# Moving one ScalarE instruction within the delta stage: a head's high half before the next head's squares, weight split and tanh

## What is computed

```
qkv = silu(causal_depthwise_conv(proj[..., :3 * DN_WIDTH], conv_w))      # 4 taps
q, k = l2_normalize(q), l2_normalize(k)                                  # 8 heads of 128
# per head, in chunks of 64 tokens in the reference:
lower = where(strict, (k * beta) @ k.T * decay, 0)
u, w  = triangular_solve(lower + I, [v * beta, k * beta * exp(gc)])
v_new = u - w @ state
o     = (q * exp(gc)) @ state + attn @ v_new
state = state * exp(gc_last) + k_dec.T @ v_new
o     = o * rsqrt(mean(o * o) + eps) * norm_w * silu(z)
y     = o @ w_out
```

## Time and profile before

| | us |
|---|---|
| median of 3 runs | 1089.87 (1088.97 to 1091.43) |
| the profiled execution | 1092.04 |
| its span, first to last instruction | 1090.2 |
| TensorE busy with matmuls | 1064.6 |
| DVE, ACT, POOL busy | 611.7, 473.7, 483.9 |

### The profile page before, as it was taken

One profiled execution on the slowest core, in us unless ns is written; L12 is line 12 of the kernel. 1 busy time (PEld: TensorE's weight loads), 2 busy tenths in 40 slices (PEclk: granted clock), 3 DMA queues, 4 the chain that ended last, 5 costly groups with the idle time before them and its releaser, 6 DMA issues. The chain is left out here.

```text
span 1090.2 us, 16275 instructions
## 1 busy us (share of the span) xinstructions
PE 1064.6 (98%) x5659; PEld 878.4 (81%) x5659; DVE 611.7 (56%) x1365; ACT 473.7 (43%) x1057; POOL 483.9 (44%) x276
## 2 busy tenths in 40 slices
PE   7999999999999999999999999999999999999997
PEld 6888888888878888888888888877788887766775
DVE  6777747767646646512122126436956767644677
ACT  6654346566543431531331333343334444454544
POOL 5786413332436775774574575346222122113230
PEclk9999999999999999999999999999999999999999
DMA  6554431221106154354343543514112011000011
GB/s 214 145 136 130 109 97 49 78 58 50 56 25 209 49 174 156 96 174 135 116 154 102 149 154 97 150 27 110 40 39 68 21 39 49 20 20 11 20 69 78
DMA packets 167157, 100.08 MB, mean 92 GB/s; under 512 B 30424, under 2 KB 160812, under 8 KB 166060
## 3 DMA queue, kind: packets, MB, share of 16 engines
q1 hardware_dynamic: 166924, 99.06, 31.3%
q10 hardware_dynamic: 160, 0.07, 0.0%
HBM read 95.69 MB, written 3.16 MB: 91 GB/s over the span
## 5 line engine op out<-in xcount | busy, mean ns | idle before, releaser
L1260 POOL TENSOR_TENSOR wlo<-stage,whi 128x1024 fp32r<-128x1024 f32 (+1 forms) x105 | 274.5, 2618 | 215.8 <-ACT whi L763 215.4
L2272 PE MATMUL ps<-hhi,whi 128*128 128x512 f32 (+1 forms) x728 | 306.9, 422 | 1.9 <-DVE gated L2033 0.9
L2272 PE MATMUL ps<-hhi,wlo 128*128 128x512 f32 (+1 forms) x728 | 296.7, 408 | 0.0
L2272 PE MATMUL ps<-hlo,whi 128*128 128x512 f32 (+1 forms) x728 | 288.5, 400 | 0.0
L2272 PEld LDWEIGHTS ps<-hhi,whi 128*128 128x128 f32 (+1 forms) x728 | 137.0, 188 | 36.1 <-issue 5.4
L1358 POOL TENSOR_TENSOR wlo<-stage,whi 128x1024 fp32r<-128x1024 f32 (+3 forms) x40 | 73.3, 1835 | 205.5 <-ACT whi L1050 205.5
L763 ACT ACTIVATE whi<-stage 128x1024 fp32r<-128x1024 f32 x104 | 109.7, 1056 | 120.7 <-PE ps L2272 88.8
L2272 PEld LDWEIGHTS ps<-hhi,wlo 128*128 128x128 f32 (+1 forms) x728 | 137.2, 188 | 30.1 <-issue 6.6
L2272 PEld LDWEIGHTS ps<-hlo,whi 128*128 128x128 f32 (+1 forms) x728 | 137.1, 188 | 26.2 <-issue 1.9
L2272 PE MATMUL ps<-ahi,whi 128*128 128x512 f32 x312 | 124.1, 398 | 3.4 <-POOL alo L1310 3.4
L1138 ACT ACTIVATE prob<-ps,aneg 128x128 f32<-128x128 f32 (+1 forms) x96 | 50.7, 528 | 168.8 <-DVE aneg L2064 122.9
(11 more groups left out here) (399 smaller groups left out, 1765.2 us busy)
## 6 DMA issues: line engine op xcount, KB each, us to landing
stage<-dn_w_in SPq DMA_DIRECT2D x32, 512.0 KB, 4.2
stage<-mlp_w_up SPq DMA_DIRECT2D x32, 512.0 KB, 4.6
stage<-mlp_w_down SPq DMA_DIRECT2D x32, 512.0 KB, 4.6
mod_w<-ada_w SPq DMA_DIRECT2D x8, 1536.0 KB, 6.6
stage<-w_in SPq DMA_DIRECT2D x17, 512.0 KB, 3.6
gcrow<-gc_rows SPq DMA_DIRECT2D x16, 256.0 KB, 3.7
stage<-dn_w_out SPq DMA_DIRECT2D x8, 512.0 KB, 3.4
stage<-w_in SPq DMA_DIRECT2D x9, 256.0 KB, 3.0
```

Of the source, the lines that this page charges most:

```text
L1260: pool.tensor_tensor(wlo[:, slot, 0:ks, 0:cols], stage[:, slot, 0:ks, 0:cols], whi[:, slot, 0:ks, 0:cols], ALU.subtract).then_inc(s["w_lo" ...
L2272: mm = pe.matmul(bank, w[:, slot, k - ks[0], 0:width], x[:, k], start=(i == 0), stop=(i == len(todo) - 1))
```

## The change

In ScalarE's order of a head, `out_hi(h - 1)` is moved in front of `q_squares(g)`, `next_split(f"v{g}")` and `conv_tanh(f"v{g}")`. It acts in heads 1 to 6: head 0 has no head before it, and head 7 has its own place for it. No instruction is added or removed, and the programs of the other engines are unchanged.

```diff
@@ -977,11 +977,11 @@
                 v_new(h, 3)
                 o_first(h, 3)
                 if ahead:
+                    if h:
+                        out_hi(h - 1)
                     q_squares(g)
                     next_split(f"v{g}")
                     conv_tanh(f"v{g}")
-                    if h:
-                        out_hi(h - 1)
                 o_squares(h, 2)
                 o_squares(h, 3)
                 if g + 1 < H:
```

## The result

The changed kernel takes 1104.86 us, median of five runs (1103.83 to 1106.38), against 1091.3 us for the kernel before (five runs, 1088.97 to 1091.56). The ratio is 1.0127, 95% interval 1.0115 to 1.0138: 1.3% slower, 13.9 us at the median of before. The profiled execution has a span of 1103.1 us, 12.9 more than before. The five runs of before have a median 1.4 us above that of the three from which the forecast was made.

A forecast was written before the change was run, and what follows sets the result against it. TensorE, its matmul row busy 1064.6 of 1090.2 us, was taken as the bound. Heads 1 to 5 (11.35 us) and head 6 (0.4) gave 11.7; 1089.87 + 11.7 = 1101.6 us, 1.1% slower, range 1096.5 to 1105.

The forecast's parts named there:

- ScalarE's order, +0.52 us: In heads 1 to 6 the moved out_hi makes squares, weight's high half and tanh each start 0.52 us later, uncovered before vT.
- The hold of vT: On DVE, vT waits for POOL's subtraction wlo, started 0.48 us earlier, taking 2.44 us instead of 0.69; 1.75 us a head.
- Heads 1 to 5, 5 x 2.27: Delta stage, heads 1 to 5: each period longer by 1.75 + 0.52 = 2.27 us, 11.35 us in all.
- Head 6, +0.4 us: In head 6 TensorE's 1.6 us loss on alo goes, but late vT opens a somewhat larger hole: +0.4 us.
- (a): Rival: vT is not held and the tanh's 0.52 us finds cover; only head 6's hole goes, 1088.3 us; chance 0.05.
- (b): Rival: no hold of vT, only the longer chain, 5 x 0.52 and head 6's -1.6 + 0.5: +1.5, 1091.4 us; chance 0.07.
- (c): Rival: vT held in every head, but the next head wins back the tanh's shift: +8.7, 1098.6 us; chance 0.08.
- (d): Rival: the edit does not act, as ScalarE waits for gf in the new place; chance below 0.01.
- the cost of the clock: Over head 0's TensorE hole the granted clock was read as staying 1.00, 2.4 GHz; the sum had no clock term.
- the upper bound of 1105: Whole kernel: at most 13.6 us lost, 6 heads at 2.27 without the 1.6 us recovered, plus the spread of before.
- The starting point, 1089.87 us: Median of three runs of the kernel before, to which the forecast added its 11.7 us.

The follow-up runs named there:

- the run with two halves: The changed kernel, but POOL makes the low half of the weight of v in two instructions of 128x512 in heads 1 to 6: 1098.92 us, ratio 1.0072.

## Why the prediction was right, and where it fell short

**ScalarE's order, +0.52 us.** Right. Alone it costs 0.54 us a head, by the run with POOL's start put late.

**The hold of vT, 1.75 us a head, out of head 0's row.** Right, by three runs: without the hold 1.73 come back, with the hold alone 1.78 are lost, and with one operand in PSUM it does not happen. vT was forecast to end 0.56 us behind wlo, and does; had all of its 0.69 us followed the release, heads would be 23.67 us long and not 23.54. That is how the prediction read the Trainium skill (SBUF — State Buffer, section SBUF: two separate sides); the measurement decides for 0.56.

**Heads 1 to 5, 5 x 2.27.** The first four are 2.24 to 2.28 us longer; the fifth is 3.13 longer, 0.85 of it the clock.

**Head 6, +0.4 us.** The stretch from 302.46 to 315.17 is 12.71 us against 12.34: +0.37. The wait on alo is gone, the one on vT stands in its place. The prediction counted only the wait on alo for TensorE in 165 to 300 us; the same view has 1.1 us on vT too, head 0's, which it had put into that head's period, so the sum is not touched.

**The rivals.** (a) gave 1088.3 us and (b) 1091.4; the run that removes the hold has (b)'s form, +1.5 us forecast and +1.5 measured by the medians (1.9 by the ratio, 0.5 to 3.2), and shows that the order without its hold would have cost about what (b) said. (c), 1098.6 us, fails by the periods, since nothing wins back the 0.52. The edit did act, so (d) fails.

**The step that failed is the cost of the clock.** I read from head 0 that the granted clock stays 1.00 over a hole of 1.2 us and put its cost at nothing; the sum had no term for it, and neither had the upper bound of 1105, made from holes and the spread of before. One head's clean row was taken for a rule, and it was one draw: behind the same hole the clock did fall in the run with POOL put late, and that head took 0.96 us more. In the two profiles the stretches I summed differ by 9.07 (heads 1 to 4), 2.28 (head 5 without the fall) and 0.37 us, 11.7 as forecast. Of the 1.2 us that the spans differ beyond it, 0.85 is the fall in head 5; the rest of the kernel, with three falls for two, is 0.65 us longer, and 0.3 goes off ahead of the heads. Over the runs, seven holes in the heads instead of two came with a mean clock of 0.992 against 0.996. An estimate from these rows: a fall of 3.4 us at half the clock lowers the mean by about 0.0015, so this is some 2.5 falls more, at 0.85 to 0.96 us each 2.1 to 2.4 us. The runs show 2.2: 13.9 less 11.7.

**The starting point, 1089.87 us.** The forecast of 1101.6 lies 3.3 us below the median of 1104.86, and the clock is only part of that. The other 1.4 us are the median of before, 1091.3 over five runs instead of 1089.87 over three. The ratio to it, 1.0127 of 1091.3, is 1105.2, just above the upper bound. By 1091.3 the same sum gives 1103.0.

## What to carry to other kernels

Before an engine's instruction is moved, look at what it was holding back on another engine: here alo, late, had kept a long POOL subtraction off the start of a DVE instruction with two SBUF operands. A head, tile or iteration in which the moved step is missing anyway (here head 0) shows the time after the change before it is made; take its whole period, and not only the one late instruction. Where a change opens repeated holes in TensorE, add a term for the clock, and look for idle time of the engine itself when an instruction has to be earlier.

## What the runs showed of the hardware

The hold is by instruction and goes both ways: behind a vT that was itself held, POOL's next 128x512 subtraction took 1.73 to 1.74 us instead of 1.27 or 1.28, in the run with two halves and in the one with POOL's order swapped. A small DVE instruction is held too: obase, 128x4, took 0.53 us instead of 0.15 beside wlo, and 0.47 beside alo in the kernel before. The hold shows in the profile as a longer record (2.44 us of vT), not as idle time.

The granted clock fell to 1.2 GHz for 3.4 us behind a TensorE hole of 1.57 us in one head of the changed kernel, and did not in the four before it and the one after it with the same hole. Runs whose holes were filled with idle products had 0.996 where the changed kernel had 0.992. One fall in the kernel before came when TensorE had been busy without a pause for over 360 us. Which hole is followed by a fall, and what brings a fall without one, stays open.
